# Strips of a chained fp32 matrix product on one core, computed in two halves of 256 tokens

## The reference, cut to what matters

```python
ab = y @ w_glu
a, b = ab[..., :dm], ab[..., dm:]
...
hm = rmsnorm(h, norm_mlp[i])
h = h + jnp.square(jax.nn.relu(hm @ w_up[i])) @ w_down[i]
gate = jax.nn.sigmoid(rmsnorm(h, norm_ple[i]) @ w_ple_gate[i])
h = h + gate * (p[i] @ w_ple_proj[i])
...
k_shared = partial_rope((hk @ w_k).reshape(bsz, seqlen, N_KV_HEADS, HEAD_DIM), pos)
v_shared = (hk @ w_v).reshape(bsz, seqlen, N_KV_HEADS, HEAD_DIM)
...
mix = swa_sink_attention(q, k_shared, v_shared, attn_sinks[j]) @ w_o[j]
...
return (o.reshape(b, s, MLA_V) * jax.nn.silu(gate)) @ w_out
```

## Time and profile before

| | |
|---|---|
| median of 3 runs | 2133.64 us (2131.75 to 2134.81) |
| span of the profiled execution | 2132.1 us |
| PE, share of the span | 92% |
| PEld | 74% |
| DVE | 46% |
| POOL | 41% |
| ACT | 34% |

### The profile page before, as it was taken

How to read it: one execution, slowest core, us unless ns; L and a number is a source line. 1 busy time by engine, 2 the same in 40 slices (tenths; PEclk the granted TensorE clock), 3 DMA queues, 4 the chain that set the end, 5 groups by cost and what they waited for, 6 DMA issues and landing times.

```text
span 2132.1 us, 24312 instructions
## 1 busy us (share of the span) xinstructions
PE 1967.1 (92%) x8728; PEld 1578.8 (74%) x8728; DVE 982.0 (46%) x1425; ACT 730.9 (34%) x1144; POOL 880.8 (41%) x495
## 2 busy tenths in 40 slices
PE   4458999999999899999999999799999999899996
PEld 3457788888888666678888888677877778576674
DVE  7559323212213858843212213844155561467544
ACT  4111434323323534443323323522233332333651
POOL 8995244444444321034444443443433334152121
PEclk8555799999999999999999999899999999899998
DMA  3124433333332220123333332222222223132011
GB/s 136 30 62 117 139 98 92 96 99 99 97 100 89 87 77 23 30 70 94 95 98 99 99 99 89 69 90 79 90 78 79 75 64 109 54 109 60 30 50 40
DMA packets 59298, 175.22 MB, mean 82 GB/s; under 512 B 14784, under 2 KB 15168, under 8 KB 58560
## 3 DMA queue, kind: packets, MB, share of 16 engines
q1 hardware_dynamic: 57344, 170.31, 26.3%
q10 hardware_dynamic: 1872, 3.80, 0.5%
HBM read 163.34 MB, written 4.19 MB: 79 GB/s over the span
## 4 chain that ended last, share of the span: by engine, by line
PE 80%; DVE 10%; POOL 8%; ACT 2%; issue 1%; DMA 0%; DVEq 0%; POOLq 0%
PE ps L831 23%; PE ps L833 22%; PE ps L832 22%; DVE h L1511 1%; PE ps L895 1%; POOL Wc L457 1%; PE ps L1166 1%; PE ps L897 1%; PE ps L964 1%; PE ps L993 1%; POOL G L453 1%; POOL G L454 1%; PE ps L1012 1%; POOL Wsn L458 1%; POOL G L455 1%
## 5 line engine op out<-in xcount | busy, mean ns | idle before, releaser
L465 POOL TENSOR_TENSOR wlo<-raw,whi 128x1024 fp32r<-128x1024 f32 x288 | 715.1, 2485 | 1203.6 <-ACT whi L498 1203.6
L498 ACT ACTIVATE whi<-raw 128x1024 fp32r<-128x1024 f32 x288 | 302.0, 1052 | 391.9 <-PE ps L833 385.5
L831 PE MATMUL ps<-Ch,whi 128*128 128x512 f32 x912 | 365.8, 401 | 13.4 <-DVE Cl L1375 11.3
L833 PE MATMUL ps<-Ch,wlo 128*128 128x512 f32 x912 | 357.3, 392 | 0.0
L832 PE MATMUL ps<-Cl,whi 128*128 128x512 f32 x912 | 357.3, 392 | 0.0
L831 PE MATMUL ps<-Ah,whi 128*128 128x512 f32 x656 | 265.5, 405 | 22.0 <-DVE Al L1375 15.9
L833 PE MATMUL ps<-Ah,wlo 128*128 128x512 f32 x656 | 256.7, 391 | 0.0
L832 PE MATMUL ps<-Al,whi 128*128 128x512 f32 x656 | 256.5, 391 | 0.0
L831 PE MATMUL ps<-Bh,whi 128*128 128x512 f32 x640 | 250.7, 392 | 0.0
L833 PE MATMUL ps<-Bh,wlo 128*128 128x512 f32 x640 | 249.0, 389 | 0.0
L832 PE MATMUL ps<-Bl,whi 128*128 128x512 f32 x640 | 249.0, 389 | 0.0
(11 more groups left out here) (343 smaller groups left out, 2494.5 us busy)
## 6 DMA issues: line engine op xcount, KB each, us to landing
raw<-in_w SPq DMA_DIRECT2D x288, 512.0 KB, 3.6
u<-in_xch SPq DMA_DIRECT2D x1, 2048.0 KB, 12.2
yg<-vsb SPq DMA_DIRECT2D x16, 128.0 KB, 2.3
yg<-z SPq DMA_DIRECT2D x16, 128.0 KB, 2.3
ysc<-yg ACTq DMA_DIRECT2D x8, 256.0 KB, 3.0
h<-in_xfm SPq DMA_DIRECT2D x2, 1024.0 KB, 5.9
out<-h SPq DMA_DIRECT2D x8, 256.0 KB, 2.0
bB<-in_bc SPq DMA_DIRECT2D x1, 1024.0 KB, 7.6
```

Of the source, the lines that this page charges most:

```text
L465: nc.gpsimd.tensor_tensor(wlo[:, r, :], raw[:, r, :], whi[:, r, :].bitcast(F32), ALU.subtract).then_inc(lo_ready, 1)
L498: nc.scalar.activation(whi[:, slot, :], raw[:, slot, :], ACT.Copy).then_inc(hi_ready, 1)
L831: nc.tensor.matmul(out, whi[:, slot, w], xh, start=first, stop=False)
L833: return nc.tensor.matmul(out, wlo[:, slot, w], xh, start=False, stop=last)
```

## The change

A function `strip_halves` is added, and `strips` calls it in place of `strip`. It works on tokens 0 to 255 with all eight weight tiles and their three products (24 matmuls of 256 columns), then on tokens 256 to 511 in the same way, into the other half of the same PSUM bank. The waits for the weights and for the bank stand ahead of both halves, those for the input tiles in the first half, and the strip's one increment comes with the last matmul of the second.

```diff
+            def strip_halves(name, l, j, x, xt, step=1):
+
+                slot, bank = (S0[name] + j) % RING, (OUT0[name] + j) % RING
+                pe.wait_ge(lo_ready, S0[name] + l + 1)
+                pe.wait_ge(evac, OUT0[name] + l - RING + 1)
+                for tokens in (slice(0, TOK // 2), slice(TOK // 2, TOK)):
+                    out = ps[:, bank, tokens]
+                    for k in range(KT):
+                        if j == 0 and tokens.start == 0:
+                            pe.wait_ge(x_lo, xt + step * k + 1)
+                        w = slice(k * P, (k + 1) * P)
+                        xh, xl = X[x][0][:, k, tokens], X[x][1][:, k, tokens]
+                        nc.tensor.matmul(out, whi[:, slot, w], xh, start=(k == 0), stop=False)
+                        nc.tensor.matmul(out, whi[:, slot, w], xl, start=False, stop=False)
+                        last = nc.tensor.matmul(out, wlo[:, slot, w], xh, start=False, stop=(k == KT - 1))
+                last.then_inc(seg_done, 1)
...
                 if between is None:
                     with pe.Fori(0, n // RING) as i:
                         for j in range(RING):
-                            strip(name, RING * i + j, j, x, xt, step)
+                            strip_halves(name, RING * i + j, j, x, xt, step)
                 else:
                     for l in range(n):
-                        strip(name, l, l, x, xt, step)
+                        strip_halves(name, l, l, x, xt, step)
                         if l == 0:
                             between()
```

## The result

The changed kernel takes 2194.76 us (median of 4 runs, 2191.47 to 2195.94) against 2133.19 us for the kernel before beside it: **slower by 2.84%** (ratio 1.0284, 95% interval 1.0268 to 1.0301). The forecast was 2192.7. The profiled execution has a span of 2189.7 us, 57.6 more than the one of before; it belongs to the fastest of the four runs, and the medians differ by 61.6.

A forecast was written before the change was run, and what follows sets the result against it. The prediction took PE's own matmul pace to bound the kernel. Its terms, 57.6 - 4.5 + 6.0 = +59.1 us, on the 2133.6 us median gave 2192.7 us, with a range of 2139 to 2240.

The forecast's parts named there:

- The pace: Common loop on PE: each whole matmul split into two halves costs 13.3 ns more, +57.6 us over 4,320 pairs.
- the excess: Common loop at full clock: 13.3 ns of each 226.7 ns matmul step beyond the 213.3 ns of 512 columns.
- by instruction: Common loop: every matmul pays 13.3 ns whatever its columns, so a pair takes 240.0 ns; the reading taken, chance 0.48.
- by column: Common loop: the 13.3 ns scale with columns, a pair stays at 226.7 ns, total 2140 us; rival, chance 0.22 (or mostly so).
- The gates: gate0 and gate1: DVE's 6.43 us a tile hides the longer strips after the first, 14 x 0.32 = -4.5 us.
- The moved waits: First strips of glu, kv, up0_0 and oout: second half comes behind the last input tile, +2.2, +2.2, +0.8, +0.7, together +6.0 us.
- load and stream in each other's way: Common loop: weight load's 112 ns and the 13.3 ns add up, +23.9 ns a pair, 2235 us; chance 0.20 shared with issue.
- excess gone: Common loop: a half takes only 112 ns, -11 us of pace, about 2129 us in total; rival, chance 0.10.
- Issue or loop ends: Common loop: issuing twice the instructions or turning 36 loop ends isn't hidden, gaps at loop ends; within a shared chance of 0.20.

The follow-up runs named there:

- the run with the gates alone: Kernel before, with halves only in the 16 strips of gate0 and gate1: 2133.42 us, ratio 0.9998.
- the two-byte view: Common loop reads the upper two bytes of each fp32r operand as bf16, ups in halves, other products whole, against the kernel before: 2129.8 us (one run).

## Why the prediction was right, point by point

- **The pace.** The term that carried the forecast, +13.3 ns for every pair, was measured at 0.120 us a half in the changed kernel, and its form (a fixed part per matmul, with the load's 112 ns as a floor beneath) held at a third size, 384 columns. It was a choice between four readings at chances of 0.48, 0.22, 0.20 and 0.10. The reason given for it, the 5 ns by which fp32 streams of 256 cycles fall behind, doesn't hold up: those 5 ns fit the floor of the weight load, since fp32r matmuls of 128 columns keep the same 112 ns with half the stream. The earlier trace rows was to rule the load out as the cause of the excess. No run confirms that: every matmul in every run has a load of its own, so a fixed cost of the load to the matmul beside it would look the same. What the runs exclude is only that load and excess add up (0.125 and over). Between by instruction and by column nothing in the trace of before decided, and it was the likelier guess that came true.
- **The gates.** -4.5 was right in its mechanism; the run with the gates alone can't be told from before. The 6.43 us of the earlier trace rows is one step of several; their mean was 6.1, still above the 5.76 of a strip.
- **The moved waits.** up0_0 and oout came out to 0.1 us. In glu the profiled pair shows 4.4 for the forecast's 2.2, as the clock fell there in one of the two executions; with unchanged code the fall alone was worth 2.6. From gate0's start to q the forecast had 3.8 and the pair shows 2.7, and that hides misses both ways: from the last tile to kv's second strip PE needed 5.4 us for 2.4, which is 3.1 more and not 2.56, as the clock was low there and the term was priced at full clock; DVE delivered that tile 0.6 us sooner, and kv's other three strips cost 0.2 more in place of 1.0. That the clock might fall more often with the halves at the waits was in the forecast's range and not in its sum; the granted clocks of the runs above suggest a few microseconds for it.
- **The total.** 59.1 forecast, 57.6 in the spans, 61.6 in the medians. Single stages of the profiled pair are off by up to 2 us either way with the clock's low stretches (glu +2.1, kv -1.1, eout and odd -2.1 where nothing was changed), so that the sum came within 1.5 us of the spans and 2.5 of the medians is better than its parts deserve: luck has a share in it.
- **Rivals.** By column, load and stream in each other's way, excess gone: each asked for another start distance (0.113, 0.125, 0.112) and none is in the trace. Issue or loop ends: PE has no idle time in 100 us with several loop ends.

## What to carry to other kernels

Read the distance between starts at full and at half clock: the difference from the plain stream shows how large an excess each matmul carries. Whether it shrinks with the columns only a second size can show, so measure one before you split: for fp32r operands it stayed at 13.3 ns, for the two-byte view it shrank. A fixed part times the added instructions is the price of a finer split. Look where an engine waits for inputs one by one: what the new order puts behind the last input is added to the critical path, and what it puts beside the earlier ones costs little, as long as what it needs for itself (here the second strip's weights) is ready.

## What the runs showed of the hardware that was not expected

- An fp32r matmul's step was N/2.4 + 13.3 ns at 512, 384 and 256 columns (226.7, 173.3, 120.0), but about 112 ns at 128 columns with a 128x128 weight load for each, and at 1.2 GHz exactly the stream: 0.427 us at 512 columns, 0.213 at 256 with the load hidden.
- Matmuls on a two-byte view with a step of two took 0.113 and 0.226 us at 256 and 512 columns, hardly less than fp32r.
- In glu's first strip, where PE waits for tiles, the mean clock from 246 to 256 us was 0.63 to 0.83 in six of ten profiled executions and 1.00 in four. Whole first strips are among both, and so is one and the same code up to there (before 1.00, gates alone 0.66), while the three with halves there are all among the six: one profile of a kernel doesn't tell where its clock falls.
